# 512-column bodies that walk K once, two alternating PSUM bank pairs, and 512-column streams for token-row outputs

## What is computed

```python
# first layer
hn = _rmsnorm(h, norm1_g)                        # [256, 2048]
q, k, v, u = split(hn @ w_in)                    # K = 2048; v is wanted token by token
h = h + concat([attn(q, k, v), s5(u)]) @ w_out   # two products with K = 1024 each
hn = _rmsnorm(h, norm2_g)
h = h + (silu(hn @ w_gate) * (hn @ w_up)) @ w_down        # width 5632
h = _rmsnorm(h, final_g)
# second layer
proj = rmsnorm(x) @ w_in                         # xr, gr, q, k, v, qm, gate logits
mk, mv = split(rmsnorm(mem) @ w_mem_kv)          # mv is wanted token by token
merged = g0 * (y_lru @ w_br_lru) + g1 * (y_attn @ w_br_attn) + g2 * (y_mem @ w_br_mem)
x = x + rmsnorm(merged @ w_out)
x = x + rmsnorm(square(relu(rmsnorm(x) @ w_up)) @ w_down)   # width 8192
```

## Time and profile before

| what | value |
|---|---|
| median of 3 runs | 3398.39 us (3397.84 to 3400.85) |
| span of the profiled execution, first to last instruction | 3399.2 us |
| TensorE matmul (PE) busy | 3279.3 us, 96% of the span |
| TensorE weight load (PEld) busy | 3212.2 us, 94% |
| VectorE (DVE) busy | 2136.7 us, 63% |
| ScalarE (ACT) busy | 1530.1 us, 45% |
| GpSimd (POOL) busy | 532.6 us, 16% |
| DMA | 580.49 MB, 171 GB/s on average |

### The profile page before, as it was taken

The page is one execution under the profiler, slowest core; times in us unless marked ns, Lnnn a source line. Parts: engine busy times, 40 slices in busy tenths (PEclk is TensorE's granted clock), DMA queues, the critical chain, the costliest instruction groups (busy, mean ns, idle before and its releaser), DMA issues.

```text
span 3399.2 us, 67239 instructions
## 1 busy us (share of the span) xinstructions
PE 3279.3 (96%) x26280; PEld 3212.2 (94%) x26280; DVE 2136.7 (63%) x2409; ACT 1530.1 (45%) x1885; POOL 532.6 (16%) x511
## 2 busy tenths in 40 slices
PE   5999999999999999899999999999997999999997
PEld 5898889999999999899999999999997999999997
DVE  7788887755555555857865666455556655555555
ACT  3444445454334344337753556444333333333342
POOL 5343443300000000703430000000014000000002
PEclk9999999999999999999999999999998999999999
DMA  6444444655555555555555444555553455555553
GB/s 212 151 154 147 156 142 143 193 184 167 194 184 180 176 182 171 162 193 173 167 195 179 154 149 161 178 174 174 181 173 118 161 186 178 187 180 186 180 185 124
DMA packets 169036, 580.49 MB, mean 171 GB/s; under 512 B 19072, under 2 KB 20864, under 8 KB 168896
## 3 DMA queue, kind: packets, MB, share of 16 engines
q1 hardware_dynamic: 160272, 558.16, 49.8%
q0 software_dynamic: 3408, 10.75, 0.9%
q10 hardware_dynamic: 5216, 9.64, 0.8%
HBM read 571.13 MB, written 7.34 MB: 170 GB/s over the span
## 4 chain that ended last, share of the span: by engine, by line
PE 87%; DVE 9%; issue 2%; ACT 2%; DMA 0%; ACTq 0%; DVEq 0%; POOL 0%; POOLq 0%; SPq 0%
PE gemm_psum L326 26%; PE gemm_psum L327 26%; PE gemm_psum L328 26%; DVE weights_lo L1104 3%; PE gemm_psum L320 1%; PE gemm_psum L321 1%; PE gemm_psum L322 1%; PE bank_b L338 1%; ACT weights_hi L688 1%; DVE projections L1375 0%; DVE x_lo L1127 0%; PE bank_s L570 0%; PE bank_b L591 0%; PE bank_s L602 0%; DVE late L1217 0%
## 5 line engine op out<-in xcount | busy, mean ns | idle before, releaser
L1104 DVE TENSOR_TENSOR weights_lo<-weights,weights_hi 128x1024 fp32r<-128x1024 f32 (+2 forms) x1104 | 1349.9, 1236 | 968.6 <-ACT weights_hi L688 962.6
L688 ACT ACTIVATE weights_hi<-weights 128x1024 fp32r<-128x1024 f32 (+2 forms) x1104 | 1109.9, 1018 | 1427.0 <-PE gemm_psum L328 1262.3
L326 PE MATMUL gemm_psum<-x_hi,weights_hi 128*128 128x256 f32 x5120 | 1467.4, 287 | 68.3 <-DVE weights_lo L1104 41.7
L327 PE MATMUL gemm_psum<-x_lo,weights_hi 128*128 128x256 f32 x5120 | 1455.9, 284 | 0.0
L328 PE MATMUL gemm_psum<-x_hi,weights_lo 128*128 128x256 f32 x5120 | 1455.5, 284 | 0.0
L326 PEld LDWEIGHTS gemm_psum<-x_hi,weights_hi 128*128 128x128 f32 x5120 | 985.2, 192 | 81.0 <-issue 37.4
L327 PEld LDWEIGHTS gemm_psum<-x_lo,weights_hi 128*128 128x128 f32 x5120 | 985.3, 192 | 0.8
L328 PEld LDWEIGHTS gemm_psum<-x_hi,weights_lo 128*128 128x128 f32 x5120 | 985.1, 192 | 0.0
L326 PE MATMUL gemm_psum<-u_hi,weights_hi 128*128 128x256 f32 x2880 | 826.0, 287 | 17.6 <-DVE weights_lo L1104 15.2
L327 PE MATMUL gemm_psum<-u_lo,weights_hi 128*128 128x256 f32 x2880 | 816.2, 283 | 0.0
L328 PE MATMUL gemm_psum<-u_hi,weights_lo 128*128 128x256 f32 x2880 | 816.1, 283 | 0.0
(11 more groups left out here) (338 smaller groups left out, 2553.6 us busy)
## 6 DMA issues: line engine op xcount, KB each, us to landing
weights<-in_w_branch SPq DMA_DIRECT2D x192, 512.0 KB, 3.3
weights<-in_w_gu SPq DMA_DIRECT2D x176, 512.0 KB, 3.4
weights<-in_w_up SPq DMA_DIRECT2D x128, 512.0 KB, 3.5
weights<-in_w_down SPq DMA_DIRECT2D x128, 512.0 KB, 3.3
weights<-in_w_dn SPq DMA_DIRECT2D x64, 512.0 KB, 3.3
weights<-in_w_in_qk SPq DMA_DIRECT2D x32, 512.0 KB, 3.3
weights<-in_w_mem_k SPq DMA_DIRECT2D x32, 512.0 KB, 3.5
weights<-in_w_mem_v SPq DMA_DIRECT2D x32, 512.0 KB, 3.4
```

Source lines behind the costliest of these rows:

```text
L326: pe.matmul(o, wh, xh[:, kk, :], start=first, stop=False)
L327: pe.matmul(o, wh, xl[:, kk, :], start=False, stop=False)
L688: act.activation(HI[:, j % RING, 0:g.kt * GC], RAW[:, j % RING, 0:g.kt * GC], ACT.Copy)\
L1104: dve.tensor_tensor(LO[:, j % RING, cols], RAW[:, j % RING, cols], HI[:, j % RING, cols].bitcast(f32), ALU.subtract).then_inc(lo_done, 1)
```

## The change

A body still makes 512 output channels, but it walks K once. A unit is `ku` K tiles by 512 columns: 2 K tiles and 24 matmuls for K of 2048, 1 K tile and 12 matmuls for K of 1024. In the last piece of the first down projection (K of 1536) a body has 6 units of 24 matmuls in place of 8 units of 18. Bytes and matmuls stay the same but for the token-row outputs, where one matmul streams 512 columns instead of two that stream 256: 672 in place of 1344. The two 256-channel parts of a body now share their end: both are read out in the events of the last slot. A body uses the bank pair that the body before it did not use, so a body waits for the read-out of the body before the last. Where a stage's first body waits for its operand piece by piece, a unit needs 2 tiles of it and not 4. The branch stage alternates a body of gates with a body of branch outputs. Loops hold two bodies where they held one.

```diff
-UNITS = 4
+BC = 2 * GC
+    def bank(self, b):
+        return 2 * ((self.first + b.c) % 2)
...
-            def units(g, b, j, operands, tokens_out=False):
-                p = j // UNITS
-                wait(pe, lo_done, b(SLOTS, SLOTS * g.first + j + 1))
-                if j % UNITS == 0:
-                    wait(pe, evac[p], b(1, g.first))
+            def arrived(g, b, j):
+                u = g.unit(b, j)
+                wait(pe, lo_done, u(1, 1))
+                if j == 0:
+                    for p in range(2):
+                        wait(pe, evac[p], b(1, g.first - 1))
+                return u.c % RING
+            def units(g, b, j, operands):
+                ring = arrived(g, b, j)
+                for n in range(4):
+                    o = GP[:, g.bank(b) + n // 2, (n % 2) * T:(n % 2 + 1) * T]
+                    for k in range(g.ku):
...
+            def token_units(g, b, j, operands):
+                for k in range(g.ku):
+                    cols = slice(k * BC, (k + 1) * BC)
+                    for t in range(2):
+                        o = GP[:, g.bank(b) + t, :]
+                        pe.matmul(o, ah, wh, start=first, stop=False)
+                        pe.matmul(o, al, wh, start=False, stop=False)
+                        mm = pe.matmul(o, ah, wl, start=False, stop=end)
...
+        def ends(g, slot):
+            return (0, 1) if g.last(slot) else ()
...
             def out_ssm_events(slot, b):
-                if slot in (3, 7):
-                    residual(out_ssm, b, slot, "norm2", 0)
+                for p in ends(out_ssm, slot):
+                    residual(out_ssm, b, p, "norm2", 0)
...
             def mem_out(scratch, g, slot, b):
-                p = slot // 4
-                wait(act, evac[p], b(1, g.first + 1))
-                act.dma_start(scratch[ix(b(2, p))].rearrange("a p k t -> p (a k) t"), mem_stage[p]).then_inc(memkv_out[p], 16)
+                for p in ends(g, slot):
+                    wait(act, evac[p], b(1, g.first + 1))
+                    act.dma_start(scratch[ix(b(2, p))].rearrange("a p k t -> p (a k) t"), mem_stage[p]).then_inc(memkv_out[p], 16)
...
-                            if j < 4:
-                                pe.wait_ge(res_lo, 2 * j + 2)
-                            if j == 4:
+                            pe.wait_ge(res_lo, j + 1)
+                            if j == 7:
                                 statistics((stat_in, 3), False)
...
-                            if j < 4:
-                                pe.wait_ge(pre_lo, j + 1)
-                            if j == 6:
+                            if j % 2 == 0:
+                                pe.wait_ge(pre_lo, j // 2 + 1)
+                            if j == 7:
                                 statistics((stat_in, 6), False)
```

389 lines of the change are left out of this document (197 added, 192 removed).

## The result

The changed kernel takes 3433.85 us (median of 4 runs, 3432.9 to 3434.78) against 3398.31 before: 1.03% slower, ratio 1.0103 with a 95% interval of 1.0089 to 1.0118. The forecast was 3408, with a range up to 3419. The sign was right, the size was 3.6 times too small: 35.5 us of loss where 9.8 were forecast.

The account below looks back on a forecast made before the run. It took TensorE to bound the kernel, busy 3279.3 of 3399.2 us, through matmul pace and 120 us of standing. Losses of 21.3 us less 11.5 of gain made +9.8 on the median: 3408 us, range 3397 to 3419.

Parts of the forecast that it names:

- `out_ssm` and the first up projection: Two residuals and a `lower` exceed TensorE's 4.3 us by 3.5 behind three bodies; fourth hidden; net +5.3 us.
- last down projection and `lru_in`: Double read-out takes 12.1 us against 8.6, a 3.5 us stall behind each of four bodies; net +4.0 us.
- attention beside `mem_k` and `mem_v`: Second read-out's DMA issue ends 0.6 us later, delaying the copies and TensorE behind it; eight heads, +4.9 us.
- two sums, start of `out2`: GpSimd sums squares of both halves before `mixed` and the kernel's end, +5.2 us; `out2`'s start, +1.2.
- start of the second feed-forward part: Root and reciprocal move to slot 7, removing a wait, -3.9 us; low clock after a stall in `mixed`, +2.0.
- token rows: In `in_v`, `mem_v` and `in_v2`, 512-column matmuls at 217.5 ns save 14.6 us, 11.5 after a deduction in `mem_v`.
- in the other feed-forward and gate stages the same doubling is hidden: There double read-outs add 0.6 to 2.8 us to 4 to 6 of the available 8.6, costing nothing.
- the first rival: Token matmuls carry their toll: at 226.2 ns the time is 3413 us, at 239.2 no gain and 3420; chance 0.2.
- The rule that prices a read-out: What `events(7)` plus one `lower` takes beyond TensorE's units 0 to 2, 4.3 or 8.6 us, is a stall.
- the longer walk absorbs the bursts: Rival: with ScalarE's copy ready and no GpSimd pressure, residual blocks nearly fit TensorE's units; 3382 us, chance 0.07.
- Double read-outs cost less: Rival: engines slip ahead while TensorE stands, or drains overlap; half of 21.3 us loss gives 3398 us; chance 0.2.
- Faster: Heading of the rival that the longer walk absorbs the bursts; its sum came to 3382 us, chance 0.07.

Follow-up runs that it names:

- e3: Changed kernel with the branch stages' gate read-outs apart, the second half two units later and ScalarE's sigmoid one after that; 3424.49 us, ratio 1.0071.
- e8: Changed kernel with an extra VectorE reciprocal behind each body's read-outs in the four down projections of the second feed-forward part; 3462.74 us.
- e5: Changed kernel with the residual read-outs of `out_ssm` and the last down projection spread in thirds over three units; 3421.93 us, ratio 1.0066.
- e9: Changed kernel with gate and memory read-outs apart, residual pieces spread over later units and ScalarE's copies one and three units behind the last slot; 3396.44 us, ratio 0.9992.
- e11: Changed kernel with narrower stationary operands in the token-row products (64, 96 or 32 columns), computing only part of those results; 3431.36 us.

## Why the prediction was right in sign and wrong in size

Term by term, forecast against measured (stage times, and the ledger where a stage holds two terms):

| term | forecast | measured |
|---|---|---|
| `out_ssm` and the first up projection | +5.3 | +12.2 |
| last down projection and `lru_in` | +4.0 | +6.7 |
| branch stages 0 and 1 | 0 | +13.1 |
| attention beside `mem_k` and `mem_v` | +4.9 | +6.8 |
| two sums, start of `out2` | +6.4 | +7.4 |
| other boundaries | +2.4 | +1.2 |
| start of the second feed-forward part | -3.9 + 2.0 | -4.9 |
| `glu`, small ones | +1.0 | +1.3 |
| token rows | -11.5 | -8 |

The forecast's -0.8 for `in_u` stands in no row; it took 0.4 us less, and 67.5 to 69.1 us over the traces of one code and the other. The measured column sums to +35.8; the first two stages and the clock in the memory stages give back some 2 us of it, which makes the 33.9 us between the spans.

- **The step that failed first** is "in the other feed-forward and gate stages the same doubling is hidden". It compared the block with the 8.6 us until `lower` of unit 3, and that comparison holds: no branch stage waits for `weights_lo`. But VectorE's and ScalarE's part of the attention stands behind that `lower` and that `upper`, and TensorE wants it at the same moment. It was priced at nothing and cost 13.1 us; e3 gives back 11.8 of them.
- **The second** is the price of a gap. The prediction priced gaps in `out_ssm` and in the last down projection by their length and the clock only in `mixed`. The gaps were sized well in `out_ssm` (3.3 us for 3.5, and +5.8 in the stage for 5.3) and too long in the last down projection: three of 3.0 and one of 3.1 for four of 3.5, so that with `lru_in` the gaps grew by 1.5 us, not by 3.7. That error hid a part of the other. The clock took 2.5 + 1.6 us in and behind `out_ssm` and 4.6 in the last down projection, where the idle time did not change at all. e8 shows that a longer gap brings it. At `mixed` it went the other way: the gap of 8.2 us came as forecast and 15 slow matmuls behind it, but 16 had stood there before, behind a gap of 5.0, and 17 behind the gap that went. The slow matmuls fell by 1.3 us where +2.0 was forecast.
- **The fourth block of `out_ssm` is not hidden** by units of 24: it stands as gaps of 0.5 and 1.9 us in the first up projection. In the five other traces of this code 0.5 to 1.6 us stand there and the third gap of `out_ssm` is 3.9 to 5.0 instead of 3.3; both stages together take 248.8 to 249.9 us in all six. That the three engines are late from the bodies before would explain it; no run tried that apart. In `lru_in` it is 3.1 us of gaps for 1.6.
- **Token rows: a term that was mis-sized**, by taking the plain float32 row, which is nearest in columns. At 226.5 ns the gain is 672 times 12.7 ns, 8.5 us before any deduction; the first rival had it. The row was also misread: the eight products of L520 in a body stand in the trace as 16 records, so that its spacing (216 ns from the unrounded starts) is that of half a matmul, and no matmul of 512 columns. It could not say what one costs.
- **The rule that prices a read-out was right as a bound and incomplete as a cause.** e5 split VectorE's block and `out_ssm` stayed at 60.3 us, because ScalarE's wait for VectorE held the next `upper`. The rival *the longer walk absorbs the bursts* named that wait, and e9 shows that it pays once the order is changed, which the change didn't do.
- Right: the drains (6.73 us for 3.9 before), the attention's waits in `mem_k` (1.0 to 1.4 us for 1.1; in `mem_v` up to 1.44 for 1.9), the gap that went at the second feed-forward part (gaps 3.5 us less for 3.9), and that the longer walk needs the second bank pair and waits for no bank. *Double read-outs cost less* is out.
- Two of the rivals' sums are off by a microsecond, without bearing on the forecast: *Faster* leaves out the 1.0 of `glu` and `out_attn` (3383), and 80.4 us less gives 3339.
- Open: why a float32r matmul costs 13 ns over its columns at 256 and at 512, and each of the two records of a plain float32 one of 256 columns only 3 over twice its columns (216 ns). e11 excludes that they shrink with the width of the load and nothing more. Open too is what decides, behind equal gaps, whether the clock falls.

## What to carry to other kernels

When two pieces of work that stood apart are joined at one place of an in-order queue, price everything that stands behind them there, not only the operation that fed TensorE last: here, in the branch stages, the block that the forecast looked at cost nothing and the attention behind `lower` 13.1 us. If the change itself frees buffers for longer, as the second bank pair did, use that at once and spread the joined work over the next units, on both engines that hand it to each other; the same operations in another order were worth 37 us. And do not add gaps up: one of 3 us can cost more than two of 1.5.

## What the runs showed of the hardware

- In the last down projection the idle time was 9.1 us in six gaps of 1.5 and in three of 3.0; the granted clock of the stage was 1.00 and 0.92. Behind gaps at which it fell, 11 to 27 matmuls ran at 1.2 GHz, 213 ns apart, 1.0 to 2.5 us per gap. In e8 four gaps of 1.79 us left it alone, and three of four gaps of 2.70 brought it down. Over fourteen traces none of 90 gaps up to 1.82 us did, 61 of 100 between 1.9 and 3.35, and all 37 from 3.7 us on.
- A float32r matmul took 119.6 ns for 256 columns and 226.5 for 512, 13 ns on top of the columns at 2.4 GHz in either case; with 32, 64 or 96 stationary columns instead of 128 it took 230 or 231.
- A plain float32 matmul of 256 columns stood in the trace as two loads and two matmuls, 216 ns apart (L520, before), 432 ns in all.
- A reciprocal on VectorE took 6.4 ns per column of 128 partitions (8.81 us for 1386, in e8), five times a subtraction's 1.2 ns (1.23 us for 1024).
